# Expert weights of a two-layer MoE block by one 4 MB transfer per matrix, in runs of 32 KB per partition, into five pairs of slots

## What is computed

```python
def expert_choice_moe(x, w_router, b_router, w_gate, w_up, w_down):
    cap = CAPACITY_FACTOR * s // N_EXPERTS                      # 64
    ...
    gate, idx = lax.top_k(aff.transpose(0, 2, 1), cap)
    xs = x[bidx, idx]
    hid = jax.nn.silu(jnp.einsum('becd,edf->becf', xs, w_gate)) * jnp.einsum('becd,edf->becf', xs, w_up)
    ys = jnp.einsum('becf,efd->becd', hid, w_down) * gate[..., None].astype(x.dtype)
    return jnp.zeros_like(x).at[bidx, idx].add(ys)
```

## Time and profile before

| | |
|---|---|
| median of 3 runs | 2578.7 us (2575.85 to 2584.68) |
| profiled execution: its own time / span | 2579.85 / 2578.0 us |
| PE busy | 2486.3 us, 96% |
| DVE / ACT / POOL busy | 45% / 19% / 5% |
| mean granted TensorE clock | 0.989 |
| read from HBM | 593.74 MB |

### The profile page before, as it was taken

One profiled execution on the slowest core, in us unless ns is written; L12 is line 12 of the kernel. 1 busy time (PEld: TensorE's weight loads), 2 busy tenths in 40 slices (PEclk: granted clock), 3 DMA queues, 4 the chain that ended last, 5 costly groups with the idle time before them and its releaser, 6 DMA issues.

```text
span 2578.0 us, 26574 instructions
## 1 busy us (share of the span) xinstructions
PE 2486.3 (96%) x10797; PEld 1504.3 (58%) x10797; DVE 1158.9 (45%) x2008; ACT 477.6 (19%) x1008; POOL 141.5 (5%) x237
## 2 busy tenths in 40 slices
PE   7999999999999999999999999899999999999899
PEld 4458888888888888555654333333455653333333
DVE  4766898655766654324842222211334641222112
ACT  2342122001322100323720000000233610000000
POOL 1311110000000000001010000000001000000000
PEclk9999999999999999999999999999999999999999
DMA  8534865541343324303058999999421159999998
GB/s 330 169 127 145 279 232 177 146 128 61 131 131 111 86 66 143 119 3 129 34 209 354 427 428 428 427 427 420 177 79 52 70 197 405 428 428 427 427 428 355
DMA packets 185034, 601.77 MB, mean 233 GB/s; under 512 B 8945, under 2 KB 123313, under 8 KB 159569
## 3 DMA queue, kind: packets, MB, share of 16 engines
q1 hardware_dynamic: 167008, 544.59, 54.6%
q0 software_dynamic: 16608, 51.22, 5.9%
q10 hardware_dynamic: 1296, 4.25, 0.4%
HBM read 593.74 MB, written 6.29 MB: 233 GB/s over the span
## 4 chain that ended last, share of the span: by engine, by line
PE 79%; DMA 15%; DVE 5%; issue 1%; ACT 1%; SPq 0%; another core or an unknown queue 0%; DVEq 0%; ACTq 0%
PE ps L2083 11%; DMA arena<-in_w_down 10%; PE ps L2652 10%; PE ps L2208 7%; PE ps L2686 6%; PE ps L2320 5%; PE ps L2094 5%; PE ps L2556 4%; PE ps L2054 3%; DMA arena<-in_w_up 3%; PE ps L2314 3%; PE ps L1954 2%; PE ps L2003 2%; PE ps L2119 2%; PE ps L1978 2%; PE ps L2697 2%
## 5 line engine op out<-in xcount | busy, mean ns | idle before, releaser
L2083 PE MATMUL ps<-arena 128*128 128x256 f32 x1280 | 277.9, 379 | 2.0 <-issue 2.0
L2083 PEld LDWEIGHTS ps<-arena 128*128 128x128 f32 x1280 | 242.6, 190 | 36.0 <-issue 3.4
L2652 PE MATMUL ps<-arena,first 128*64 128x512 f32 x1024 | 231.4, 593 | 11.1 <-DMA arena<-in_w_up 11.0
L2652 PE MATMUL ps<-arena 128*64 128x512 f32 x1024 | 232.2, 595 | 1.8 <-DMA arena<-in_w_up 1.8
L2686 PE MATMUL ps<-arena 128*64 128x512 f32 x896 | 209.4, 625 | 23.1 <-DMA arena<-in_w_down 21.7
L2208 PE MATMUL ps<-arena 128*128 128x256 f32 x896 | 193.8, 379 | 0.1
L2208 PEld LDWEIGHTS ps<-arena 128*128 128x128 f32 x896 | 170.1, 190 | 23.6 <-issue 0.5
L2652 PEld LDWEIGHTS ps<-arena,first 128*64 128x64 f32 x1024 | 73.3, 137 | 160.5 <-issue 136.6
L2686 PEld LDWEIGHTS ps<-arena 128*64 128x64 f32 x896 | 68.4, 143 | 161.2 <-issue 159.5
L2652 PEld LDWEIGHTS ps<-arena 128*64 128x64 f32 x1024 | 73.6, 137 | 140.0 <-issue 133.2
L2094 PE MATMUL ps<-arena 128*128 128x256 f32 x672 | 147.9, 382 | 3.0 <-DVE arena L1316 3.0
(11 more groups left out here) (454 smaller groups left out, 3191.0 us busy)
## 6 DMA issues: line engine op xcount, KB each, us to landing
arena<-in_w_gate SPq DMA_DIRECT2D x64, 2048.0 KB, 36.5
arena<-in_w_up SPq DMA_DIRECT2D x64, 2048.0 KB, 35.3
arena<-in_w_down SPq DMA_DIRECT2D x54, 2048.0 KB, 34.5
arena<-in_ffn_w SPq DMA_DIRECT2D x24, 2048.0 KB, 9.2
arena<-in_w_mod POOLq DMA_DIRECT2D x80, 512.0 KB, 5.1
arena<-in_ffn_w SPq DMA_DIRECT2D x32, 1024.0 KB, 7.3
arena<-in_w_down SPq DMA_DIRECT2D x16, 1024.0 KB, 37.4
arena<-in_w_in SPq DMA_DIRECT2D x10, 1536.0 KB, 12.0
```

Of the source, the lines that this page charges most:

```text
L2083: ins = mm(ps[:, i % 6, 0:256], src[:, k, P * j:P * j + P], x[:, k, :], start=(k == 0), stop=(k == 3))
L2652: ins = mm(ps[CAP * half:CAP * half + CAP, bank, :], xsT[q][:, k, CAP * (e % 2):CAP * (e % 2) + CAP], wv[:, k, 512 * half:512 * half + 512 ...
```

## The change

The rows of a matrix are laid out anew: row 8p + k on partition p, so that a partition reads 32 KB in one run. Half q of a matrix is now k = 4q to 4q + 3 on each partition (still 16 KB each). To match, the hidden features are split as 8p + 4h + j: column half h of gate and up is no longer 512 neighbours but 128 groups of 4, each 8 values after the last (`inner`). The transposes of the gathered rows step by 8 values instead of 4, and the gains of the norm (`gperm`) follow.

The slots form five pairs, (6,8), (7,9), (0,1), (2,3), (4,5). The first eleven loads are still halves, wait for the same events in the same order, but hold other halves (`FIRST`). The twelfth still goes to slot 10, which is then no longer used in the layer. Matrix 6 comes as two halves; matrices 7 to 45 come whole (`load_whole`), 4 MB by one transfer into a pair, which waits until both of its slots are free. Down e0 now comes whole ahead of down e1. The last two matrices come in the same small pieces as before.

```diff
-        ORDER = (10, 2, 1, 4, 3, 8, 7, 5, 0, 6, 9)
-        LOADS = 6 * EXPERTS
...
+        MATS = 3 * EXPERTS
+        FREED = (10, 2, 1, 4, 3, 8, 7, 5, 0, 6, 9)
+        FIRST = (10, 6, 8, 7, 9, 0, 1, 2, 3, 4, 5, 10)
+        PAIRS = ((6, 8), (7, 9), (0, 1), (2, 3), (4, 5))
+
+        def half_slot(m, q):
+            return FIRST[2 * m + q] if m < 6 else PAIRS[(m - 6) % 5][q]
+
+        def is_whole(m):
+            return 7 <= m < MATS - 2
+
+        def land_slot(m, q):
+            return half_slot(m, 0 if is_whole(m) else q)
...
+                def load_whole(m):
+
+                    s = half_slot(m, 0)
+                    slot_free(m, 0)
+                    slot_free(m, 1)
+                    sp.dma_start(at(RING2_AT[s], 2 * SLOT), matrix(m)).then_inc(r2_in[s], 16)
...
-                for n in range(LOADS - 4):
-                    load(n)
-                for n in (LOADS - 4, LOADS - 3):
-                    load(n)
+                for s in FREED:
+                    load_first(FIRST.index(s))
+                load_eleventh()
+                for q in range(2):
+                    load_half(6, q)
+                for m in range(7, MATS - 2):
+                    load_whole(m)
...
-                                ins = mm(ps[CAP * half:CAP * half + CAP, bank, :], xsT[q][:, k, CAP * (e % 2):CAP * (e % 2) + CAP], wv[:, k, 512 * half:512 * half + 512],
+                                ins = mm(ps[CAP * half:CAP * half + CAP, bank, :].rearrange("c (n j) -> c n j", j=4),
+                                         xsT[q][:, k, CAP * (e % 2):CAP * (e % 2) + CAP],
+                                         wv[:, k, :].rearrange("p (n j) -> p n j", j=KC)[:, :, 4 * half:4 * half + 4],
                                          start=(q == 0 and k == 0), stop=(q == 1 and k == 3))
```

More of the change, by code:

```diff
@@ new lines, in land_count, with use_count, land_total, use_total @@
+        def land_count(s, m, q):
+            n = 0
+            for i in range(2 * m + q + 1):
+                mm, qq = divmod(i, 2)
+                if land_slot(mm, qq) == s and not (is_whole(mm) and qq):
+                    n += 2 if i == 11 else 1
+            return n
+        def use_count(s, m, q):
+            return sum(2 if i == 0 else 1 for i in range(2 * m + q + 1) if half_slot(*divmod(i, 2)) == s)
+        def land_total(s):
+            return land_count(s, MATS - 1, 1)
+        def use_total(s):
+            return use_count(s, MATS - 1, 1)
@@ L358, in load_number, with half_of @@
+        def half_of(e, part):
             i, par = divmod(e, 2)
-            return 12 * i + (4 * par + part if part < 4 else 8 + 2 * (part - 4) + par)
+            return 6 * i + (2 * par + part // 2 if part < 4 else 4 + par), part % 2
         def part_used(l, e, part):
-            s, _, done, _ = expert_load(l, load_number(e, part))
-            return r2_used[s], done
+            m, q = half_of(e, part)
+            s = half_slot(m, q)
+            return r2_used[s], l * use_total(s) + use_count(s, m, q)
@@ L457, in _ @@
                         sp.dma_start(ring2[s][:, 3072:3648], uq[:, s - 1, :]).then_inc(r2_in[s], 16)
[L459 to L494, removed]
+                def matrix(m):
+                    i, j = divmod(m, 6)
+                    w = a[("w_gate_2", "w_up_2")[j % 2] if j < 4 else "w_down_2"][l, 2 * i + (j // 2 if j < 4 else j - 4)]
+                    return w.rearrange("(p k) n -> p (k n)", k=KC)
@@ new lines, in slot_free, with load_first @@
+                def slot_free(m, q):
+                    s = half_slot(m, q)
+                    sp.wait_ge(r2_used[s], l * use_total(s) + use_count(s, m, q) - 1)
+                def load_first(n):
+                    m, q = divmod(n, 2)
+                    s = FIRST[n]
+                    name, value = {10: ("conv_ps", 6 * l + 6), 0: ("wout_ps", 24 * l + 24), 1: ("q_ps", 3 * l + 3), 2: ("p2_ps", 16 * l + 16),
+                                   3: ("o_ps", 18 * l + 18), 4: ("sc_done", 12 * l + 12), 5: ("wout_ps", 24 * l + 16),
+                                   6: ("lgp_ps", 4 * l + 4), 7: ("wout_ps", 24 * l + 8),
+                                   8: ("t_ps", 2 * l + 2), 9: ("xn_saved", 64 * l + 64)}[s]
+                    sp.wait_ge(sm[name], value)
+                    if s == 9:
+                        sp.wait_ge(got[0], 16 * (8 * l + 1))
+                    sp.dma_start(ring2[s], matrix(m)[:, SLOT * q:SLOT * q + SLOT]).then_inc(r2_in[s], 16)
@@ new lines, in load_eleventh, with load_half @@
+                def load_eleventh():
+                    s = FIRST[11]
+                    for k in range(2):
+                        sp.wait_ge(r2_used[s], l * use_total(s) + 1 + k)
+                        sp.dma_start(ring2[s][:, 2048 * k:2048 * k + 2048], matrix(5)[:, SLOT + 2048 * k:SLOT + 2048 * k + 2048]).then_inc(r2_in[s], 16)
+                def load_half(m, q):
+                    s = half_slot(m, q)
+                    slot_free(m, q)
+                    sp.dma_start(ring2[s], matrix(m)[:, SLOT * q:SLOT * q + SLOT]).then_inc(r2_in[s], 16)
@@ L496, in _, with load_rest @@
+                def load_rest(par, q, landed, lo, hi):
+                    s = half_slot(MATS - 2 + par, q)
+                    w = matrix(MATS - 2 + par)[:, SLOT * q + 2048:SLOT * q + SLOT].rearrange("p (k n) -> p k n", k=2)
+                    sp.dma_start(ring2[s][:, 2048:].rearrange("p (k n) -> p k n", k=2)[:, :, lo:hi], w[:, :, lo:hi]).then_inc(landed, 16)
                 if l:
-                    sp.wait_ge(r2_used[5], loads_before(5, LOADS))
+                    sp.wait_ge(r2_used[5], use_total(5))
@@ L503, in _ @@
                 sp.dma_start(ring2[0].rearrange("p (k n) -> p k n", k=4), w_out[:, 2:6, :]).then_inc(r2_in[0], 16)
[L504 to L507 removed]
+                for s in FREED:
[5 more added lines that the diff above has]
+                    load_whole(m)
                 for par in range(2):
[L509 to L511 removed]
+                    load_last(par, 0)
                 for par in range(2):
[L513 removed]
+                    load_rest(par, 0, r1_in[2 + par], 0, D)
                 for par in range(2):
[L515 removed]
+                    load_last(par, 1)
+                for par in range(2):
+                    load_rest(par, 1, r1_in[par], 0, 512)
+                for par in range(2):
+                    load_rest(par, 1, last_cols_in[par], 512, D)
             for half in range(2):
@@ L2640, in piece @@
                 def piece(e, part):
-                    s, landed_at = part_in(l, e, part)
-                    pe.wait_ge(r2_in[s], landed_at)
+                    s, landed, landed_at = part_in(l, e, part)
+                    pe.wait_ge(landed, landed_at)
                     return ring2[s].rearrange("p (k n) -> p k n", k=4), r2_used[s]
```

27 lines of the change are left out of this document (14 added, 13 removed).

## The result

The changed kernel takes 2588.26 us (median of 5 runs, 2585.59 to 2590.78) against 2578.7. The ratio is 1.0036, 95% interval 1.0024 to 1.0047, that is 9.3 us, between 6.2 and 12.1. The profiled execution took 2585.59 us with a span of 2583.8.

A forecast was written before the change was run, and what follows sets the result against it. DMA was taken as the bound in the MoE parts, PE having 7.0 us to spare per pair. Terms 4.4 + 6.4 + 2.0 - 5.3 = +7.5 us gave 2586 us on the median, range 2577 to 2598.

The forecast's parts named there:

- Longer runs: Weight loads in both MoE layers: 32 KB runs save an 8.5 ns packet cost each, 5.3 us in all.
- DMA stands still at the start: Start of each layer's MoE: matrices 7 and 9 wait for slots PE frees late, so DMA idles; 4.4 us in all.
- the upper end of 11: Upper bound for DMA idling at the start of both layers, 11 us, from a 5.4 us gap.
- behind this nothing idles: After the gaps at matrices 7 and 9, later loads such as 10 and 15 get slots in time; no further loss.
- PE works longer after the last landing of up: Layer end: both halves of the last expert's up are multiplied after one landing; 3.2 us a layer, 6.4 in all.
- A cold clock before the last gate: PE waits 5 to 6 us before `outer`, then runs partly at 1.2 GHz; 1.0 us a layer, 2.0 in all.
- Groups of four: `inner` reading the moving operand in groups of four costs nothing; rival of slow reading up to 2975 us, chance 0.10.
- Slot 10 idle, transfers of 4 MB in the queue: Load queue 20 MB deep instead of 22; slots still free in time, so the cost is hidden.
- Each transfer costs its start: Rival: every queued load pays 2.8 us beside its bytes, so fewer transfers give 218 us back, 2368 us; chance 0.01.

The follow-up runs named there:

- PE kept awake: Changed kernel plus ten idle matmuls of 256 columns on PE in the wait ahead of `outer`, last two full pairs of each layer; 2584.91 us, 1.0027 to before.
- all by halves: Changed kernel with every matrix loaded as two 2 MB transfers in 16 KB runs, slot 10 still idle; 2579.75 us, 1.0001 to the kernel before.
- both ends by halves: Changed kernel with matrices 7, 8, 9 and 40 to 45 loaded by halves, 30 a layer staying whole; 2577.45 us, 0.999 to the kernel before.

## Why the prediction was right, and where it wasn't

The sign, the size and the mechanism hold: 7.5 us forecast over the median, 9.3 measured with 6.2 to 12.1; in the MoE parts of the traces alone, 6.8. By its steps:

- *Longer runs*, -5.3. The changed kernel's long stretches carry 0.81% more than those of the kernel before in layer 0 (142.15 against 141.01 MB from 1440 to 1770 us) and 0.65% more in layer 1 (124.74 against 123.94 from 2210 to 2500). Of 383 us that is 3.1 and 2.5, -5.6 in all. The two full queues, 4 KB and 16 KB, gave nearly the right cost per packet: (9.79 - 9.71) us over the 8 packets of 32 KB of each engine is 10 ns against 8.5.
- *DMA stands still at the start*, +4.4. Measured 1.4 + 2.5 = 3.9, at the two matrices named: matrices 7 and 9 land 10.7 and 11.5 us behind the ones ahead of them in layer 0, 11.5 and 12.0 in layer 1, where 9.7 is the pace. The sum came nearer than its parts, 2.6 and 1.8 us, and that is luck: in layer 0 the first `outer`, which frees slot 3, took 15.65 us before and 13.95 after, at full clock, and matrix 9 was issued 42.1 us behind the start of the MoE part instead of 43.9. Five traces with this start lie between 3.3 and 6.5 us in all, under the upper end of 11. The step "behind this nothing idles" held in the changed kernel, though by little: as soon as the start is repaired, matrix 15 idles.
- *PE works longer after the last landing of up*, +6.4. Measured 2.8 a layer with PE kept awake, 5.6 in all. What the prediction didn't see is that this term and the cold clock sit on lines of work of nearly equal length: it added them as if either could be undone alone. Undoing this one alone brought nothing. The sum holds all the same, since both lines are in it.
- *A cold clock before the last gate*, +2.0. The wait ahead of `outer` is 6.2 and 5.2 us (5 to 6 forecast), the clock behind it 0.63, PE 1.7 and 0.6 us late at the last up (1.1), and keeping PE awake gave 2.1 back.
- *Groups of four*: nothing, as taken. 592 to 594 ns an instruction, and 0.9996 for the kernel with the layout alone. The page SBUF — State Buffer of the Trainium skill, "Specifications (TRN2)", wants two hits on each 16-byte line. These runs bear the direction out: four float32 of a line in a row run at full rate, one of a line at half; two of a line, which meet its two hits, still cost 5%.
- *Slot 10 idle, transfers of 4 MB in the queue*: nothing; the kernel with all by halves shows it for the slot. For the deeper queue of whole transfers no run tells it apart from the rest.
- *Each transfer costs its start* (2368 us) fell: 39 transfers fewer a layer brought 2.5 to 3.1 us, which is no more than the packets' saving. The rule of the Trainium skill's page SBUF — State Buffer, section "The DMA setup-cost knee", charged to each transfer, isn't borne out in this queue, where transfers of 4 MB land 9.71 us apart and those of 2 MB 4.89.

The measured terms add up to 3.9 + 5.6 + 2.1 - 5.6 = +6.0, against +6.8 in the MoE parts of the traces. The two profiled executions differ by 5.7. The medians differ by more, 9.6. The two traces also differ by -2.8 us ahead of the MoE, by +1.5 between its layers and by +0.3 behind it, parts that the change doesn't touch. So the 4 us between the terms and the medians are within what executions differ by, and weren't settled. The forecast of 7.5 lies between the two; that it misses the measured ratio by only 1.8 us says little about its terms.

Open is also why the stream keeps less of the longer runs when the ends go by halves: matrix 15 explains 0.6 to 2.7 us a layer. In the kernel with both ends by halves there are also single landings that come 1.6 to 2.4 us later than the pace (at 1516, 1765 and 2459 us), behind loads that had been queued for 20 us and more. What they are isn't known: the changed kernel has one like them at 2459 us, and its DMA moves 429 GB/s from 2447 to 2461 us.

## What to carry to other kernels

In a stream that is bound by DMA, ask of a larger transfer what it costs at both ends: it can start only when all of its slot is free, and can be used only when all of it has landed. Small transfers at the ends took the 9.3 us back here. Large ones in the middle, where only the packets' cost counts, then brought 2.6 us, between 0.3 and 4.9, at the edge of what could be told. Add up such costs only after asking whether they lie on one line of work or on two: of two lines that end together, mending one brings nothing. And a gap that comes from slots freed late moves to the next slot that is freed late, when it is closed.

## What the runs showed of the hardware

- A moving operand in fp32 that takes every fourth value is read at half rate (28.95 against 13.88 us for 64 instructions of 512 columns, two column halves side by side), every second value 5% slower (14.57), and groups of four with gaps of four at full rate.
- In a full queue, transfers of 2 MB in runs of 16 KB landed 4.89 us apart and transfers of 4 MB in runs of 32 KB 9.71 us apart: 427 against 430 or 431 GB/s.
- In the changed kernel the eight `outer` that had waited 4.1 to 6.7 us for DMA took 15.3 to 17.0 us instead of 13.95; behind one of them the granted clock was 0.63 in the mean over 5 us. With 4.5 us of idle matmuls in such a wait, the two `outer` with 1.1 and 1.2 us of waiting left took 13.95 us (granted clock 1.00 behind the first), the two with 2.3 and 2.4 us left 15.5 and 15.7.
